# Starting two transformer blocks chunk by chunk: modulation tiles in pairs, four weight units at once, and two changed seams

## The reference, cut to what matters

```python
c_act = silu(c)                                   # 1024 values
mod = c_act @ w_ada + b_ada                       # 6 x 1024: sh1, sc1, ga1, sh2, sc2, ga2
xn = rms_norm(x, g_mix) * (1 + sc1) + sh1         # first norm: scale sc1, shift sh1
proj = xn @ w_in + b_in                           # first products: indexer queries, keys, weights, q
...
h = h + ga2 * (act @ w_down)                      # end of block one
h = rms_norm(h, g_final)                          # its last norm ...
u = rms_norm(concat(meta, h), attn_norm)          # ... and at once the first norm of block two
...
h = h + act2 @ w_down_2                           # end of block two
out = rms_norm(h, final_norm)[:, 16:]
```

## Time and profile before

| what | value |
|---|---|
| median of three runs | 1833.76 us (1833.09 to 1834.21) |
| the profiled execution | 1833.9 us, its span 1832.1 us |
| TensorE matmul busy | 1765.4 us (96%) |
| GpSimd / VectorE / ScalarE busy | 1473.2 / 1046.9 / 528.1 us |
| mean granted TensorE clock | 0.983 |
| first product of `gp` with XN starts | 41.84 us after the span's start |

### The profile page before, as it was taken

One profiled execution on the slowest core, in us unless ns is written; L12 is line 12 of the kernel. 1 busy time (PEld: TensorE's weight loads), 2 busy tenths in 40 slices (PEclk: granted clock), 3 DMA queues, 4 the chain that ended last, 5 costly groups with the idle time before them and its releaser, 6 DMA issues.

```text
span 1832.1 us, 33487 instructions
## 1 busy us (share of the span) xinstructions
PE 1765.4 (96%) x11364; PEld 1563.4 (85%) x11364; DVE 1046.9 (57%) x1658; ACT 528.1 (29%) x778; POOL 1473.2 (80%) x2245
## 2 busy tenths in 40 slices
PE   4999998999999999999899999999999999999997
PEld 2767775577799999888799999999999999999885
DVE  6457897956767666611457656655764455555101
ACT  3245663320121111100434443443343211111000
POOL 1758995478999999999578867876886899999885
PEclk8899999999999999999999999999999999999999
DMA  8333323444422232333122222222222322332332
GB/s 323 92 124 87 100 87 117 138 148 150 149 92 92 92 90 85 99 105 112 60 81 73 79 70 81 71 70 79 81 70 70 93 92 92 95 100 92 104 103 92
DMA packets 54301, 184.44 MB, mean 101 GB/s; under 512 B 6673, under 2 KB 7857, under 8 KB 54226
## 3 DMA queue, kind: packets, MB, share of 16 engines
q1 hardware_dynamic: 48690, 169.20, 29.3%
q10 hardware_dynamic: 5536, 14.16, 2.3%
HBM read 178.62 MB, written 4.72 MB: 100 GB/s over the span
## 4 chain that ended last, share of the span: by engine, by line
PE 56%; POOL 26%; issue 10%; DMA 4%; DVE 1%; SPq 1%; POOLq 1%; ACT 0%; ACTq 0%; DVEq 0%
PE gp L387 17%; PE gp L388 17%; PE gp L389 17%; POOL Wlo L378 17%; POOL Whi L375 6%; POOL probe L374 4%; DMA raw<-units 3%; PE A L716 2%; DMA AW<-ada 1%; PE A L763 0%; SPq L323 0%; PE A L712 0%; PE A L765 0%; PE A L744 0%; PE A L756 0%
## 5 line engine op out<-in xcount | busy, mean ns | idle before, releaser
L378 POOL TENSOR_TENSOR Wlo<-raw,Whi 128x256 fp32r<-128x256 f32 x1120 | 973.1, 889 | 46.7
L387 PE MATMUL gp<-XNhi,Whi 128*128 128x264 f32 (+3 forms) x2736 | 851.8, 311 | 31.5 <-DVE XNlo L1122 23.8
L388 PE MATMUL gp<-XNlo,Whi 128*128 128x264 f32 (+3 forms) x2736 | 837.7, 306 | 0.0
L389 PE MATMUL gp<-XNhi,Wlo 128*128 128x264 f32 (+3 forms) x2736 | 834.7, 305 | 0.0
L387 PEld LDWEIGHTS gp<-XNhi,Whi 128*128 128x128 f32 x2736 | 518.9, 190 | 70.7 <-POOL Wlo L378 18.1
L388 PEld LDWEIGHTS gp<-XNlo,Whi 128*128 128x128 f32 x2736 | 519.3, 190 | 25.0 <-issue 2.2
L389 PEld LDWEIGHTS gp<-XNhi,Wlo 128*128 128x128 f32 x2736 | 518.5, 189 | 23.6
L374 POOL TENSOR_TENSOR probe<-raw 1x1 f32<-1x1 f32 x560 | 179.0, 320 | 291.4 <-PE gp L389 248.6
L375 POOL TENSOR_SCALAR Whi<-raw 128x512 fp32r<-128x512 f32 x560 | 347.0, 620 | 0.0
L387 PE MATMUL gp<-AChi,Whi 128*128 128x512 f32 x352 | 137.3, 390 | 0.4 <-POOL Wlo L378 0.4
L389 PE MATMUL gp<-AChi,Wlo 128*128 128x512 f32 x352 | 137.0, 389 | 0.0
(11 more groups left out here) (311 smaller groups left out, 2246.3 us busy)
## 6 DMA issues: line engine op xcount, KB each, us to landing
raw<-units SPq DMA_DIRECT2D x280, 512.0 KB, 3.5
AW<-ada SPq DMA_DIRECT2D x16, 512.0 KB, 8.8
AWL<-ada SPq DMA_DIRECT2D x16, 512.0 KB, 4.3
AWL<-ada ACTq DMA_DIRECT2D x16, 512.0 KB, 4.3
bias_rows<-RB ACTq DMA_DIRECT2D x1, 2560.0 KB, 15.0
H<-xT SPq DMA_DIRECT2D x1, 2048.0 KB, 8.5
BIAS<-bias_rows ACTq DMA_DIRECT2D x1, 2048.0 KB, 8.9
out<-H SPq DMA_DIRECT2D x8, 256.0 KB, 2.1
```

The costliest lines, as they stand in the source:

```text
L378: ins = pool.tensor_tensor(lo[:, c:c + UNIT // 4], src[:, c:c + UNIT // 4], hi[:, c:c + UNIT // 4].bitcast(F32), ALU.subtract)
L387: pe.matmul(dst, Whi[s][:, k, :], rhi, start=start, stop=False)
L388: pe.matmul(dst, Whi[s][:, k, :], rlo, start=False, stop=False)
L389: return pe.matmul(dst, Wlo[s][:, k, :], rhi, start=False, stop=stop)
```

## The change

**Start.** SyncE loads x in four pairs of chunks, each with a semaphore of its own, and then the `w_ada` tiles in the order scale 0, shift 0, scale 1, shift 1, and so on; weight units 0 to 3 are issued between them, behind tiles 1, 3, 11 and 13. The squares of x are summed on VectorE, so TensorE has two stat matmuls instead of eight. VectorE makes x * rstd (`spread`, into `XS`) and reduces the tiles of a chunk (`rows`); the scale and shift of a chunk are formed alone, and ScalarE applies them twice, to `nt` and to `XNhi`. The shifts of chunks 2, 4, 6 and 7 are not reduced on VectorE: their tiles come transposed, and TensorE multiplies each of the eight 128x128 blocks with one column of silu(c) (`shift`). Four weight units have split tiles of their own and take chunk j as it comes, units 2 and 3 four and six chunks behind; the split of units 0 to 3 waits for no release. The large copy of the bias rows is issued behind the chunks.

**Seam.** The weighted square moves from ScalarE to VectorE and carries the epsilon term, so the two matmuls with the epsilon matrix go; the fused sum stands first, and the logarithm of the other (`RST1`) moves into the first head of block two, which is written out of the loop. `norm_split` makes the low part of a chunk before the scaled form of the chunk two on.

**End.** The second and third unit of the last output chunk are multiplied for the first 256 tokens and then for the last 256; sum, inverse root, scaling and stores go by token halves, and stores by pairs of chunks.

```diff
+FRONT = 4
+LAG = (0, 0, 4, 6)
+ROW_SHIFTS = (0, 1, 3, 5)
+COL_SHIFTS = (2, 4, 6, 7)
...
+            for j in range(ADA_FIRST):
+                if j >= ADA_SLOTS:
+                    before = j - ADA_SLOTS
+                    if before % 2 == 0 or before // 2 in ROW_SHIFTS:
+                        sp.wait_ge(ada_done, ADA_SLOTS + rows_before(before + 1))
+                    else:
+                        sp.wait_ge(shift_mm, before + 1 - rows_before(before + 1))
+                chunk = (KC if j % 2 == 0 else 0) + j // 2
+                sp.dma_start(AW[j % ADA_SLOTS][:, :], ada[chunk, :, :]).then_inc(ada_in[j % ADA_SLOTS], 16)
+                if j in (1, 3, 11, 13):
+                    load_unit((1, 3, 11, 13).index(j))
...
+            pe.matmul(A67[:, 0:S], mean, SQS[:, 0:S], start=True, stop=False)
+            pe.wait_ge(sq_ready, KC)
+            pe.matmul(A67[:, 0:S], mean, sq[:, (KC - 1) % 2, 0:S], start=False, stop=True).then_inc(stat_mm, KC)
...
+            def shift(n):
+
+                j = 2 * COL_SHIFTS[n] + 1
+                w = AW[j % ADA_SLOTS]
+                pe.wait_ge(ada_in[j % ADA_SLOTS], 16 * (j // ADA_SLOTS + 1))
...
+                for k in range(KC):
+                    mm = pe.matmul(A67[:, (1 - n % 2) * 512 + n:(1 - n % 2) * 512 + n + 1], w[:, k * P:(k + 1) * P], CC[:, k:k + 1],
+                                   start=(k == 0), stop=(k == KC - 1))
+                mm.then_inc(shift_mm, 1)
...
+            for j in range(KC + LAG[-1]):
+                if j + 1 in COL_SHIFTS:
+                    shift(COL_SHIFTS.index(j + 1))
+                if j < KC:
+                    pe.wait_ge(xn_ready, j + 1)
+                for u in range(FRONT):
+                    if 0 <= j - LAG[u] < KC:
+                        front_block(u, j - LAG[u])
...
+            rows(0)
+            dve.wait_ge(rstd_ready, 1)
+            spread(0)
+            for k in range(KC):
+                dve.drain()
+                dve.scalar_tensor_tensor(AB1[:, k:k + 1], MOD[:, KC + k:KC + k + 1], SCB[:, k:k + 1], vec("g_mix", k), ALU.add, ALU.mult)
+                if k in ROW_SHIFTS:
+                    dve.tensor_tensor(MOD[:, k:k + 1], MOD[:, k:k + 1], vec("b_ada", k), ALU.add)
+                else:
+                    n = COL_SHIFTS.index(k)
+                    dve.wait_ge(shift_mm, n + 1)
...
+                dve.drain().then_inc(mod_ready, 1)
+                if k + 1 < KC:
+                    spread(k + 1)
+                    rows(k + 1)
+                dve.wait_ge(nt_ready, k + 1)
+                dve.wait_ge(xhi_ready, k + 1)
+                dve.tensor_tensor(XNlo[:, k, META:T], nt[:, k % 3, 0:S], XNhi[:, k, META:T].bitcast(F32), ALU.subtract).then_inc(xn_ready, 1)
...
-                    if m == FUSED:
-                        pe.matmul(A45[:, 0:n], eps_mean, part[0][:, 0:n], start=total, stop=False)
...
+                    if m == FUSED:
+                        dve.scalar_tensor_tensor(SQG[:, c, :], hk, GE[:, bass.ds(i * 2 + c, 1)], hk, ALU.mult,
+                                                 ALU.mult).then_inc(sqg_ready, 1)
...
+                if first:
+                    act.wait_ge(stat_mm, KC + FUSED)
+                    act.activation(RST1[:, :], A67[:, 0:S], ACT.Ln, bias=EPSC)
...
+            for j in (1, 2):
+                for k in range(min(KC, FC - j * KC)):
+                    split_wait(u + j, k)
+                    mm = last_block(0, j, k)
+            mm.then_inc(last_mm, 1)
+            for k in range(KC):
+                last_block(1, 1, k)
+            pe.wait_ge(rstd_ready, 4)
+            pe.wait_ge(sums_ready, (KC - 1) * 4)
+            last_stats(0)
+            for k in range(FC - 2 * KC):
+                mm = last_block(1, 2, k)
+            mm.then_inc(last_mm, 1)
+            last_stats(1)
```

More of the change, by code:

```diff
@@ L71, with rows_before @@
 ADA_SLOTS = 8
+FRONT = 4
+LAG = (0, 0, 4, 6)
+ROW_SHIFTS = (0, 1, 3, 5)
+COL_SHIFTS = (2, 4, 6, 7)
+ADA_ROWS = KC + len(ROW_SHIFTS)
+def rows_before(n):
+    return sum(1 for j in range(n) if j % 2 == 0 or j // 2 in ROW_SHIFTS)
 VEC = {}
@@ L383, in _ @@
+            for u in range(FRONT):
+                split(u // 2, u % 2, u, None)
+            for s in range(2):
+                split(FRONT // 2, s, s, 2)
+            with pool.Fori(FRONT // 2 + 1, UNITS // 2) as i:
+                for s in range(2):
+                    split(i, s, s, 0)
         @block.tensor
@@ new lines, in front_block @@
+            def front_block(u, k):
+                split_wait(u, k)
+                if u == FRONT - 1 and k == 0:
+                    pe.wait_ge(meta_rstd, 1)
+                mm = three(gp[u % 2][:, (u // 2) * 512:(u // 2) * 512 + S], u, k, XNhi[:, k, META:T], XNlo[:, k, META:T], k == 0, k == KC - 1)
+                if k == KC // 2 - 1:
+                    mm.then_inc(half_done, 1)
+                if k == KC - 1:
+                    mm.then_inc(unit_done, 1)
+            pe.wait_ge(gp_free[0], 1)
@@ L1088, in _ @@
+            head(0, 0, first=True)
+            head(0, 1)
+            with act.Fori(1, KC // 2) as i:
+                head(i, 0)
+                head(i, 1)
             norm_stats(3)
@@ L1183, in residual @@
                         chunk(i, c)
+                if m == 4:
+                    add(KC // 2 - 1, 0)
+                    chunk(KC // 2 - 1, 0)
+                    add(KC // 2 - 1, 1)
+                    for t in range(2):
+                        hk = H[:, KC - 1, META + t * HALF:META + (t + 1) * HALF]
+                        dve.wait_ge(last_mm, t + 1)
+                        dve.tensor_tensor(hk, gp[1][:, t * 512:t * 512 + HALF], hk, ALU.add).then_inc(h_ready, 1)
             dve.memset(ONES[:, :], 1.0).then_inc(row_ready, 1)
@@ new lines, in _, with row, rows @@
+            dve.wait_ge(v_in, 16)
+            dve.tensor_scalar(SCB[:, :], vec("b_ada", KC, KC), 1.0, None, ALU.add)
+            dve.wait_ge(silu_c, 1)
+            def row(j, column):
+                w = AW[j % ADA_SLOTS]
+                dve.wait_ge(ada_in[j % ADA_SLOTS], 16 * (j // ADA_SLOTS + 1))
+                dve.tensor_tensor_reduce(w[:, :], w[:, :], CS[:, :], 1.0, 0.0, ALU.mult, ALU.add, column).then_inc(ada_done, 1)
+            def rows(k):
+                row(2 * k, MOD[:, KC + k:KC + k + 1])
+                if k in ROW_SHIFTS:
+                    row(2 * k + 1, MOD[:, k:k + 1])
```

434 lines of the change are left out of this document (245 added, 189 removed).

## The result

The changed kernel takes 1838.97 us (median of 12 runs, 1832.2 to 1844.07) and the kernel before, on the same chips, 1834.28 (12 runs, 1831.13 to 1836.65). The ratio is 1.0023, with a 95% interval of 1.0015 to 1.0032: slower by 3 to 6 us, across the 0.2% that the forecast's three cases are cut at. 1834.6 was forecast. 1838.97 lies inside the range of 1822 to 1841, near its upper end, but outside the 1831 to 1837.5 that the forecast gave to its own sum, in a part that it gave to rival C alone. What stands out beside the median is the spread: 12 us from fastest to slowest, against 5.5 before. Two executions were profiled, of 1835.15 us and (experiment 12) of 1839.35 us, and the second is the typical one.

What follows compares the result with a forecast made beforehand. Matmuls fill 96% of the span, so only TensorE's waits and lower-clock time can be won. Start +6.0, seam -3.7, end -1.5 give +0.8, 1834.7, taken as 1834.6 us with the median 0.1 lower; own range 1831 to 1837.5, wide 1822 to 1841.

Steps and rivals of the forecast that it cites:

- three cases: Whole kernel: faster 0.32, same 0.43, slower 0.25; same means within 0.2% (3.7 us).
- rival C: Start: VectorE and GpSimd stand in each other's way, 5.4 us more than charged, 1840 in all; chance 0.25.
- The start, +6.0 forecast: Start of the kernel: four weight units done at 80.8 us instead of 74.8, 6.0 us later.
- rival A: Start: the clock rises during chunk 4 or 5, four units done at 76 to 78, total about 1831; chance 0.12.
- The price of a shift: Start, TensorE: 16 passes for each shift, 3.4 us at the lower clock, bounded at 1.9 at the upper.
- Rival B: Start: shifts are cheap (total 1827.8) or the clock is up all the way (about 1821); chance 0.25.
- The forecast's sign for it: Start: VectorE's tile-reduction rows above 1.7 would show rival C.
- thirteen operations: Start: large VectorE operations on the chain, five before chunk 0, four each for chunks 2 and 4; 4 us charged.
- The seam, -3.7 forecast: Seam between the blocks: product starts 3.1 us earlier, with clock and logarithm terms a gain of 3.7 (2.5 to 5.5).
- The 1.0 for the clock: Seam: TensorE's shorter gap is followed by less time at the lower clock; 1.0 us gained (0 to 2.7).
- The 0.4 for RST1's logarithm: First head after the seam: the logarithm delays the chain to level 1 by up to 0.7; 0.4 us charged.
- The end, -1.5 forecast: End: 10.5 us instead of 13.5 behind the last product, which comes 1.5 later; gain 1.5 (0.5 to 2).

Runs made afterwards that it cites:

- experiment 12: The changed kernel run and profiled once more, with no further edit; 1839.35 us, one run.
- aligned kernel: The changed kernel plus two unused tiles (96 and 64 bytes a partition) so that AChi begins at 114816; 1836.61 us, ratio 1.0010.
- seam and end alone: The kernel before with only the seam's and the end's parts of the diff, AChi at 114816; 1830.08 us, ratio 0.9983.
- filled kernel: The aligned kernel plus 26 unread 512-column matmuls in TensorE's gaps before chunks 0, 2 and 4; 1830.17 us, ratio 0.9977.

## Why the prediction was right in its range and wrong in its sum

**The start, +6.0 forecast.** The mechanism and its size hold. Aligned kernel against seam and end alone, same place of the tiles: 1836.61 - 1830.08 = 6.5 us, or 5.0 by the two ratios (1.0010 and 0.9983). In the second profile the first product came at 29.7 (29.0 forecast), chunk 2 at 40.4 (40.4), chunk 5 at 58.7 (58.5), chunk 6 at 65.9 (65.7), four units done at 80.6 (80.8; the forecast's own terms give 80.7). That they fit to 0.2 us is in part luck. The forecast has every matmul up to chunk 6 at the lower level. In this profile the first shift (2.06 us), chunk 1 and the first microsecond of chunk 4 were at the upper one, which made up for the 0.7 at the first product and for VectorE's work on chunks 2 and 4, 5.9 and 5.6 us instead of 5.4 and 4.9. In the first profile, at the lower level until chunk 2, chunk 2 came at 41.7. Not every run is like the second: rival A, the clock rising in chunk 4, is what the first profile shows (four units at 74.8), and it is neither right nor wrong but a matter of the run. TensorE has three gaps in the start, of 2.8 to 9.0 us, and the level at which it comes out of one is not the same in each run: before chunk 4 it waited 2.81 us in the first profile and 2.93 in the second, and the first matmul behind took 0.80 us (lower level) in the one and 0.50 (upper) in the other. The aligned kernel was at the upper level in chunk 3 and met chunk 4 at the lower:

```profile
51.50:72.00 20.50, 19.19 (x61) 16.52 (x62) 8.89 (x22) 4.56 (x6) 2.44 (x4) 0.51 0.24 86
```

Marks of 122.9, 128.8 and 130.5 for one and the same start give 0, 5.9 and 7.6 us, a spread as wide as half of the scatter of the runs. VectorE waited for each of the four shifts, 6.1 us in all in the first profile, so the chain is the one that was told (in the aligned profile the second shift, at the upper level, was waited for by nobody). The forecast gave A and B chances as if one level had to hold in every run.

**The price of a shift**, 3.4 us at the lower and at most 1.9 at the upper level: 3.40 and 3.41 measured, and 1.84. Rival B, cheap passes, falls. The Trainium skill's 107 ns for loading 128 columns (TensorE: Matmul & The Clock Gate, section LDWEIGHTS) is near 0.115, the pass at the upper level, and half the 0.21 at the lower.

**Rival C.** The forecast's sign for it came in: VectorE's reductions took 1.75 us in the median of the first profile, above 1.7. Its price did not. On the thirteen operations that the forecast counted, the first profile shows 5.5 us over their lengths alone (0.69 and 1.22), where 4 were charged and C decides above 6.9; no instruction waited for a whole subtraction. That the chunks came near their times all the same is a balance of errors: VectorE's stretch for chunk 2 took 5.5 us in the first profile, 5.4 forecast, as the forecast set the small operations (0.6, measured 0.3) and the lengths alone too high. The time landed where only C was to bring it, above 1837.5, but by another cause, the place of the tiles.

**The seam, -3.7 forecast.** -2.2 to the first product instead of -3.1: the weighted square on VectorE took 0.97, not 0.75, and the statistic's matmul waited 0.55 for it, so rstd came 1.8 earlier, not 2.4; and the split is 0.4 instead of 0.7 earlier. The 1.0 for the clock isn't borne out. The first `h_sig` wait is 14.6 us behind the first product in the first profile, 15.1 in the second and 15.3 in the kernel before, but it is 14.6 too in the kernel before with 32 unused bytes, whose seam is the old one. So a shorter gap is not shown to give clock back; this stretch differs by 0.7 us from run to run. The 0.4 for RST1's logarithm didn't show: from there to the wait for `M2lo` it is 507.8 us in the kernel before and 507.9 in both profiles. The seam by rows is -2.2.

**The end, -1.5 forecast.** Last product to the end of the span 10.5 (10.5). The 132 halved matmuls with the sum between them take 16.7 us where 66 whole ones took 15.0, 1.7 more (1.5). Together -1.3. Seam and end by themselves measured 3.7 in the median, 3.5 by these rows.

**The term that was missing.** The sum failed at a step that isn't in it: that the matmuls of the two down products, 528 in each, keep their pace. They lost 2.4 and 3.1 us, where the forecast, without a word, has nothing. It was not to be had from the trace of before, but it was in the diff: tiles declared ahead of `AChi` move it and its neighbours. The Trainium skill (SBUF — State Buffer, section Operand start alignment) says that its rule on starts is about legality, that nothing was timed; here the time changes at starts that are all legal.

**What stays open.** 6.5 - 3.7 + 5.4 is 8.2, and 4.7 was measured. The aligned kernel should then be 5.4 below the changed one and is 2.4 below. The profiles, cut at the same points, show two places where runs differ (us; the first stretch ends at the mark, "block two" runs from its first product to the start of the second down product):

| stretch | before | changed, first | changed, second | aligned |
|---|---|---|---|---|
| start | 122.9 | 122.9 | 128.8 | 130.5 |
| to the first down product | 634.5 | 633.8 | 630.1 | 632.8 |
| first down product | 120.6 | 123.0 | 123.0 | 120.8 |
| seam | 11.2 | 9.0 | 9.0 | 9.0 |
| block two | 809.8 | 809.7 | 811.6 | 811.4 |
| second down product | 119.5 | 124.4 | 124.4 | 121.3 |
| end | 13.7 | 10.7 | 10.7 | 10.7 |

The start is one. The other is the second row, whose code the change leaves alone: in the fourteen profiles of this case it takes 630.1 to 635.6 us, whatever the start. Some 2.6 of the 3.7 us between the two profiles of the changed kernel lie behind one wait of TensorE for `MB`, 3.3 us in both: 36.1 us to the same later matmul in the first, 33.6 in the second. Behind it the first profile is at the lower level for some 5 us and the second at the upper throughout:

```profile
418.90:424.00 5.10, 5.09 (x12) 4.03 (x13) 4.58 (x7) 0.00 (x0) 2.15 (x2) 0.50 0.63 227
```

```profile
423.70:428.80 5.10, 5.10 (x22) 4.18 (x23) 4.66 (x6) 0.00 (x0) 4.05 (x6) 1.00 0.78 244
```

So the second profile lost 5.9 us at the start and got 3.7 back in the middle. A difference of 2 to 4 us between medians of 5 to 12 runs can come from either place, and the missing 3.5 us were not traced to one. Nor is it shown why `AChi` at 114688 has another pace than at 114816: only the places differ, and no rule for them was found. It isn't the moving tile's own place alone. In block one's FFN the moving tiles `XNhi` and `XNlo` and the weights lie at the same bytes in every kernel here, and still the changed kernel and the aligned one, which differ in nothing but two unused tiles, do 338 and 342 matmuls in 40 us:

```profile
545.00:585.00 40.00, 40.00 (x338) 40.00 (x337) 27.89 (x45) 8.19 (x11) 38.83 (x55) 1.00 0.25 92
```

```profile
545.00:585.00 40.00, 40.00 (x342) 40.00 (x342) 28.48 (x49) 8.26 (x11) 38.83 (x55) 1.00 0.30 92
```

Which of the moved tiles sets the pace, there or in the down products, no run separates.

## What to carry to other kernels

When a diff changes what is allocated ahead of a large tile, count the new addresses as an edit of their own, and compare the pace of untouched matmuls before reading anything else: 32 bytes were worth more here than the seam and the end together. When work is put on TensorE for another engine's next step, place it in a gap before the matmuls that it would otherwise follow: one line made 10.8 us in the median (8.2 at the mark in the profiles), and the changed kernel with it and with `AChi` back at 128 over a multiple of 256, at 1825.8 us (0.9960 of the kernel before), is the best measured here. Where TensorE has gaps, forecast the clock as a spread and not as a level, judge by many runs, and compare the stretches that the change leaves alone before a difference is put down to the one that it touches.

## What the runs showed of the hardware

- A 512-column matmul with its weights loaded behind the one before took 0.2267, 0.2323 or 0.2333 us at the upper clock level, with the moving tiles (and the rest of the stage's tiles) at other places and the weights at the same ones: 0.2267 with the tile at 115072 and 114816, 0.2323 at 114688, 0.2333 at 115104 and 114656. Which of the moved tiles does it is open: matmuls whose moving tile and weights stayed in place took 0.117 or 0.118 (342 or 338 in 40 us).
- One pass of an f32 matmul with 128x128 weights and a single column: 0.21 us at the lower level, 0.115 at the upper.
- Behind a wait of TensorE of 3.3 us for the same instruction the same kernel was at the lower level for some 5 us in one run and at the upper in another, 2.6 us apart.
- Fillers can win the clock and lose it again: 0.98 from 29 to 49 us, 0.52 from there to 69. In the filled kernel the fastest run was 1818.8 and the slowest 1837.1 us.
- A VectorE reduction over 1024 columns takes 1.22 us alone and 1.73 with GpSimd splitting beside it, a subtraction of 512 columns 0.69 and 0.94.
